# A diffusion transformer layer: turned rows beside turned activations, gathers three ahead, context first in the band group, router on rows that are not normalised

## What is computed

```python
def layer(x, cond):                      # once for the context tokens, once for the latent ones
    sh1, sc1, gt1, sh2, sc2, gt2 = split(silu(cond) @ w_ada + b_ada, 6)
    h = rms_norm(x, g_pre_attn) * (1 + sc1) + sh1
    qa, ka, va, qb, kb, vb = split(h @ w_in)         # 8 + 8 query heads, 2 + 2 key heads of 64
    qa, ka = rope(rms_norm(qa, g_qa)), rope(rms_norm(ka, g_ka))
    oa = attention(qa, ka, va)           # global: a latent token reads 512 latent keys + 128 cached
    ob = windowed(qb, kb, vb, sink)      # band of +-128 tokens + 128 cached keys, with a sink logit
    x = x + gt1 * rms_norm(concat(oa, ob) @ w_out, g_post_attn)
    h = rms_norm(x, g_pre_ffn) * (1 + sc2) + sh2
    aff = softmax(h @ w_router)                      # 16 experts
    g, idx = top_k(aff.T, cap)                       # cap 64 latent rows, 16 context rows an expert
    y = (silu(h[idx] @ w_gate) * (h[idx] @ w_up)) @ w_down * g
    return x + gt2 * rms_norm(scatter_add(y), g_post_ffn)
```

## Time and profile before

| | |
|---|---|
| median of the runs shown | 989.94 us |
| the profiled execution's own time | 991.05 us |
| its span in the profile | 989.2 us |
| PE busy | 916.5 us (93% of the span) |
| DVE, ACT, POOL busy | 336.8, 211.5, 125.4 us |
| mean DMA rate | 270 GB/s, 267 MB in all |
| mean granted TensorE clock | 0.966 of full speed |

### The profile page before, as it was taken

How to read it: one execution, slowest core, us unless ns; L and a number is a source line. 1 busy time by engine, 2 the same in 40 slices (tenths; PEclk the granted TensorE clock), 3 DMA queues, 4 the chain that set the end, 5 groups by cost and what they waited for, 6 DMA issues and landing times.

```text
span 989.2 us, 20007 instructions
## 1 busy us (share of the span) xinstructions
PE 916.5 (93%) x8581; PEld 451.1 (46%) x8581; DVE 336.8 (34%) x887; ACT 211.5 (21%) x497; POOL 125.4 (13%) x207
## 2 busy tenths in 40 slices
PE   3699999899999999459999999999999999999995
PEld 2345544677755555333444434443444344444431
DVE  2255534777877762731101110111011101110115
ACT  5122221567655541210000000000000000000002
POOL 1011100000000000021202220222022202220021
PEclk9899999799999998679999999999999999999998
DMA  9996340500000007839999999999999999999782
GB/s 361 352 378 221 140 170 1 208 1 2 2 1 23 22 23 295 321 137 352 353 403 393 393 395 407 393 393 394 408 393 392 393 409 393 392 391 411 289 292 107
DMA packets 77780, 267.09 MB, mean 270 GB/s; under 512 B 6360, under 2 KB 12040, under 8 KB 77736
## 3 DMA queue, kind: packets, MB, share of 16 engines
q1 hardware_dynamic: 65536, 247.61, 64.2%
q0 software_dynamic: 7088, 14.95, 5.8%
q10 hardware_dynamic: 5112, 3.93, 1.2%
HBM read 252.32 MB, written 14.16 MB: 269 GB/s over the span
## 4 chain that ended last, share of the span: by engine, by line
PE 55%; DVE 2%; ACT 1%; issue 0%; DMA 0%; POOL 0%; DVEq 0%; ACTq 0%
PE ps L747 33%; PE ps L759 17%; PE ps L725 1%; PE ps L794 1%; PE ps L789 1%; PE ps L832 0%; PE ps L827 0%; PE ps L727 0%; PE ps L664 0%; DMA reg<-rows_c,kt 0%; ACT reg L1056 0%; DVE ring L1502 0%; ACT ring L1098 0%; DVE kt L1396 0%; DVE ring L1509 0%
## 5 line engine op out<-in xcount | busy, mean ns | idle before, releaser
L747 PE MATMUL ps<-ring,reg 128*32 128x512 f32 x2048 | 231.2, 592 | 0.0
L759 PE MATMUL ps<-ring,reg 128*32 128x256 f32 x2048 | 124.1, 384 | 3.2 <-DVE reg L1455 2.2
L747 PEld LDWEIGHTS ps<-ring,reg 128*32 128x32 f32 x2048 | 66.5, 110 | 126.7 <-issue 116.0
L1470 DVE TENSOR_SCALAR reg<-ps,kt 128x512 f32<-128x512 f32 x15 | 11.3, 751 | 317.5 <-PE ps L747 317.5
L511 PE MATMUL ps<-ring,reg_qt 128*128 128x512 f32 x240 | 107.5, 602 | 6.5 <-DMA ring<-in_w_in 6.5
L759 PEld LDWEIGHTS ps<-ring,reg 128*32 128x32 f32 x2048 | 65.1, 111 | 68.2 <-issue 31.0
L1073 ACT ACTIVATE reg<-ps 128x256 f32<-128x256 f32 x16 | 6.1, 383 | 404.1 <-PE ps L789 404.1
L641 PE MATMUL ps<-ring,reg 128*128 128x512 f32 x160 | 78.8, 621 | 0.0
L511 PEld LDWEIGHTS ps<-ring,reg_qt 128*128 128x128 f32 x240 | 45.1, 193 | 60.1 <-issue 52.9
L1545 POOL TENSOR_TENSOR small<-small,mhalf 128x1 f32<-128x1 f32 (+2 forms) x30 | 23.0, 766 | 349.9 <-DVE small L1302 240.9
L1026 ACT ACTIVATE ring<-ps 128x640 f32<-128x640 f32 (+3 forms) x80 | 44.3, 553 | 67.7 <-PE ps L572 65.5
(11 more groups left out here) (200 smaller groups left out, 984.8 us busy)
## 6 DMA issues: line engine op xcount, KB each, us to landing
ring<-in_w_up SPq DMA_DIRECT2D x32, 2048.0 KB, 18.4
ring<-in_w_down SPq DMA_DIRECT2D x32, 2048.0 KB, 17.8
ring<-in_w_gate SPq DMA_DIRECT2D x16, 2048.0 KB, 15.7
reg_qt<-in_w_gate SPq DMA_DIRECT2D x16, 2048.0 KB, 16.1
ring<-in_w_ada SPq DMA_DIRECT2D x12, 2048.0 KB, 15.0
reg<-in_x_sample SPq DMA_DIRECT2D x8, 512.0 KB, 6.2
ring<-in_w_in SPq DMA_DIRECT2D x2, 2048.0 KB, 14.0
ring<-in_w_out SPq DMA_DIRECT2D x2, 2048.0 KB, 10.0
```

What stands on the lines that cost most here:

```text
L747: last = pe.matmul(o[64 * n + r:64 * n + r + 32, :], x[:, j, hf, r:r + 32], w[:, j, n * HALF:(n + 1) * HALF], start=(hf == 0 and j == 0), ...
L759: last = pe.matmul(o[32 * q:32 * q + 32, :], x[:, c % 2, c // 2, :], w[:, j, q * QUART:(q + 1) * QUART], start=(c == 0), stop=(c == KC - 1))
L1470: dve.tensor_scalar(y_l, ps[:, 3, :], g_l[:, bass.ds(e, 1)], None, ALU.mult)
```

## The change

Eight edits, in the order in which they run:

1. The small loads move from ACT's queue to SP's: seven ("keys") behind the first block of w_in, ten ("consts") behind the second. The first block of w_in comes in four DMAs and is awaited in two halves. `ADA_AFTER` moves its pieces one to two projections later.
2. `shift_to_logits` and `spread_shift` form the part of the logits that comes from the shift, and DVE folds the scale into the router's weights (`wrm`), so that logits = rstd * (x1 @ wrm) + bias. The signs are turned, so that a minimum takes the place of the maximum.
3. Group A runs four pairs of latent units and then one pair of context units, four times.
4. `OUT_ORDER` becomes 0, 1, 2, 3, 4. PE turns x1 itself, not the normalised rows; ACT copies it (`copy_x1`) where DVE modulated it. `route_logits` of three tiles moves into the units.
5. Each tile has its own softmax. The context's top 16 and its lists come before the last tile's norm. The last tile (latent 4) is squared, gated, added, turned and copied in halves. POOL takes over the means.
6. The latent top 64 runs after the last tile's affinities. On PE `cast_gate(1, ...)` stands ahead of the last `turn_aff`.
7. In an expert's step `turn_rows(e + 2)` follows the turned activations, so twelve transposes stand together; gathers run three experts ahead; DVE's `modulate` stands after `activations`.
8. `last_context` moves between the two halves of the last down product.

```diff
-ADA_AFTER = {2: 2, 5: 3, 8: 4, 11: 5}
+ADA_AFTER = {4: 2, 7: 3, 9: 4, 12: 5}
-OUT_ORDER = [1, 2, 3, 4, 0]
-HEAD_UNITS = ([(0, h, t) for t in range(TILES) for h in range(HEADS)]
+OUT_ORDER = [0, 1, 2, 3, 4]
+A_PAIRS = []
+for quarter in range(4):
+    A_PAIRS += [(2 * p, 1 + quarter) for p in range(PAIRS)] + [(2 * quarter, 0)]
+HEAD_UNITS = ([(0, h + i, t) for h, t in A_PAIRS for i in (0, 1)]
...
                     if m == 0:
-                        sp.dma_start(d[:, :, 0:256], w[:, :, 512:768]).then_inc(slot_in[slot_of(u)], 16)
-                        sp.dma_start(d[:, :, 256:512], w[:, :, 1280:1536]).then_inc(slot_in[slot_of(u)], 16)
+                        for b in (0, 1):
+                            k = slice(4 * b, 4 * b + 4)
+                            sp.dma_start(d[:, k, 0:256], w[:, k, 512:768]).then_inc(win0_in[b], 16)
+                            sp.dma_start(d[:, k, 256:512], w[:, k, 1280:1536]).then_inc(win0_in[b], 16)
+                        load_keys()
...
+                        if m == 1:
+                            load_consts()
...
+            def shift_to_logits():
+
+                pe.wait_ge(consts_in, 16 * N_CONSTS)
+                pe.wait_ge(modcol_ready, 4)
+                for c in range(KC):
+                    last = pe.matmul(ps[0:E, 7, 0:2], wr[:, c * E:(c + 1) * E], cmod[:, 2, :, c],
+                                     start=(c == 0), stop=(c == KC - 1))
+                last.then_inc(shift_turned, 1)
...
+                if o >= 2 and j == 7:
+                    route_logits(o - 2)
             turn_probs(n_units - 1)
             values(n_units // 2 - 1)
 
             project_out(4, 0, KC)
-            for o in range(3):
-                route_logits(o)
             turn_x1(3, 0)
+            turn_x1(3, 1)
+            turn_aff(0)
             project_out(4, KC, KC + 4)
-            turn_x1(3, 1)
+            route_logits(3)
+            turn_aff(1)
+            turn_aff(2)
             project_out(4, KC + 4, 2 * KC)
-            route_logits(3)
...
+            turn_aff(3)
+            pe.wait_ge(lists_c_ready, 1)
+            for a in (2, 3):
+                last = pe.transpose(ps[:, 1, a * E:(a + 1) * E], lists[:, a, :], ident[0:E, 0:E])
+            last.then_inc(lists_c_turned, 1)
             turn_x1(4, 0)
             turn_x1(4, 1)
             route_logits(4)
...
             for r in range(4):
                 cast_gate(1, r)
+            turn_aff(4)
...
                 product_l(2, U, xT_l[odd]).then_inc(up_a, 1)
-                if not final:
-                    turn_rows(e + 1)
                 weight_in(3, e)
...
                 if following:
                     pe.wait_ge(xe_ready, e + 2)
                     gate_product(*following, 0)
+                pe.wait_ge(y_ready, e + 1)
                 for j in range(2):
-                    last = pe.transpose(TC[:, QUART + j * P:QUART + (j + 1) * P], a_c[:, j * P:(j + 1) * P],
+                    last = pe.transpose(YC[:, QUART + j * P:QUART + (j + 1) * P], a_c[:, j * P:(j + 1) * P],
...
+                if ahead:
+                    pe.wait_ge(xe_ready, e + 2)
+                    turn_rows(e + 2)
                 if following:
                     gate_product(*following, 1)
-                pe.wait_ge(y_ready, e + 1)
...
                     product_l(4, Y, aT_l).then_inc(down_a, 1)
+                    last_context()
                     product_l(5, Y, aT_l).then_inc(down_b, 1)
...
             gate_product(0, 0, 0)
+            turn_rows(1)
             gate_product(0, 0, 1)
...
+            square_half(0)
+            exp_logits(3)
+            square_half(1)
+            square_x1_half(0)
+            square_x1_half(1)
             normalise_x1(4)
             store_rows(4)
...
+            def copy_x1_last(half):
+                o = TILES - 1
                 t = OUT_ORDER[o]
...
+                dve.wait_ge(x1_turned, 2 * o + half + 1)
+                dve.wait_ge(x1_squared, o + 2)
+                dve.tensor_copy(h2T[:, 4 * half:4 * half + 4, t * P:(t + 1) * P],
+                                out_at(o)[:, half, :].rearrange("p (c n) -> p c n", c=4)).then_inc(h2_ready, 1)
...
+            gate_half(1)
+            add_half(0)
+            add_half(1)
+            copy_x1_last(0)
+            copy_x1_last(1)
+            logits_of(4)
+            affinities(4)
+            dve.wait_ge(aff_turned, 2)
+            link(dve.tensor_copy(affs[0][:, LAT - P:LAT], ps[0:E, 7, 0:P]))
             for r in range(CAP_L // 8):
...
                 for odd in (0, 1):
-                    modulate(pair * 2 + odd + 1, 1 - odd)
                     activations(pair * 2 + odd)
+                    modulate(pair * 2 + odd + 2, odd)
                     weigh(pair * 2 + odd)
...
-            pool.wait_ge(xe_turned, 1)
-            gather(1)
+            for n in (1, 2):
+                pool.wait_ge(xe_turned, n)
+                gather(n)
...
-            with pool.Fori(0, E - 2) as e:
-                pool.wait_ge(xe_turned, e + 2)
-                gather(e + 2)
+            with pool.Fori(0, E - 3) as e:
+                pool.wait_ge(xe_turned, e + 3)
+                gather(e + 3)
                 scatter(e)
+            scatter(E - 3)
             scatter(E - 2)
```

More of the change, by code:

```diff
@@ L330, in build @@
         N_EARLY = 6
-        N_CONSTS = 17
-        LOADS = [sum((2 if UNITS[v][:2] == ("win", 0) else 1) for v in range(len(UNITS)) if slot_of(v) == s)
-                 for s in range(SLOTS)]
+        N_KEYS = 7
+        N_CONSTS = 10
+        LOADS = [sum(UNITS[v][:2] != ("win", 0) for v in range(len(UNITS)) if slot_of(v) == s) for s in range(SLOTS)]
         block = ctx.enter_context(nc.Block())
@@ L444, in landed @@
             def landed(u):
-                loads = sum((2 if UNITS[v][:2] == ("win", 0) else 1) for v in range(u + 1) if slot_of(v) == slot_of(u))
+                loads = sum(UNITS[v][:2] != ("win", 0) for v in range(u + 1) if slot_of(v) == slot_of(u))
                 pe.wait_ge(slot_in[slot_of(u)], 16 * loads)
@@ L643, in project_out @@
                                      start=(c == 0), stop=(c == KC - 1))
+                    if i == KC - 1 and o == TILES - 1:
+                        last.then_inc(o_half, 1)
                     if i == 2 * KC - 1:
@@ L666, in route_logits @@
-                last.then_inc(router_done, 1)
+                    pe.wait_ge(router_set, 3)
+                if o == TILES - 1:
+                    pe.wait_ge(logits_ready, o)
+                for c in range(KC):
+                    if c % 4 == 0:
+                        pe.wait_ge(h2_ready, 2 * o + (1 + c // 4 if o == TILES - 1 else 2))
+                    last = pe.matmul(dst, h2T[:, c, t * P:(t + 1) * P],
+                                     wrm[:, (KC * cond + c) * E:(KC * cond + c + 1) * E], start=(c == 0),
+                                     stop=(c == KC - 1))
@@ new lines, in route_logits, with turn_aff @@
+                last.then_inc(router_done, 1)
+            def turn_aff(o):
+                t = OUT_ORDER[o]
+                pe.wait_ge(aff_ready, o + 1)
+                if t in (0, 1):
+                    pe.wait_ge(exp_done, n_units)
+                if t == TILES - 1:
+                    pe.wait_ge(attn_ready, n_units // 2)
+                dst = ps[0:E, 1, 0:P] if t == 0 else ps[0:E, 7, 0:P] if t == TILES - 1 else ps[0:E, 0, (t - 1) * P:t * P]
+                last = pe.transpose(dst, expl[:, t, :], ident[:, :])
+                if t == 0:
+                    last.then_inc(aff_c_turned, 1)
+                if t >= TILES - 2:
+                    last.then_inc(aff_turned, 1)
@@ L706, in _ @@
             route_logits(4)
[L707 to L708 removed]
             for r in range(4):
                 cast_gate(1, r)
+            turn_aff(4)
             pe.wait_ge(lists_ready, 1)
[L712 to L713 removed]
+            for a in (0, 1):
+                last = pe.transpose(ps[:, 0, a * E:(a + 1) * E], lists[:, a, :], ident[0:E, 0:E])
             last.then_inc(lists_turned, 1)
@@ L771, in gate_product, with last_context, expert @@
                 product_l(s, G, xT_l[odd]).then_inc((gate_a, gate_b)[half], 1)
-            def expert(e, odd, following, final=False):
+            def last_context():
+                pe.wait_ge(put_on_ready, 1)
+                pe.wait_ge(y_copied_c, 1)
+                pe.wait_ge(silu_done, 2 * E)
+                pe.wait_ge(actT_l_ready, E)
+                for q in range(4):
+                    last = pe.matmul(ps[:, (0, 1, 2, 5)[q], 0:QUART], put_on_c[32 * q:32 * q + 32, :],
+                                     y_c[32 * q:32 * q + 32, :], start=True, stop=True)
+                last.then_inc(put_on, 1)
+            def expert(e, odd, following, ahead=True, final=False):
                 weight_in(2, e)
```

355 lines of the change are left out of this document (205 added, 150 removed).

## The result

| | before | after |
|---|---|---|
| median | 990.42 us | 976.89 us |
| lowest to highest | 989.48 to 991.17 | 975.98 to 979.38 |
| profiled execution, its span | 991.05, 989.2 us | 975.98, 974.2 us |
| mean granted clock | 0.966 | 0.981 |

The ratio is 0.9868, with a 95% interval of 0.9847 to 0.9888: 13.5 us faster, against 11.8 forecast.

What follows compares the result with a forecast made beforehand. PE was taken to bound projections, group B's projection stretch and experts (loads also near their limit there), small-step chains the rest. Terms -7.3 + 1.0 + 0.5 + 0.2 + 5.5 - 5.0 - 3.9 - 2.8 = -11.8 gave 978.1 us median, range 974 to 983.

Steps and rivals of the forecast that it cites:

- B: Rival at the start: the start doesn't move, 4 us of gain instead of 7.3 or less, 983; chance 0.15.
- C: Rival in the experts: the loads bind, so nothing is gained in the loop, 982; chance 0.15.
- D: Rival in the routing: it runs at full clock, -3.3 us more, 975; chance 0.15.
- Rival A: In attention: the clock falls at the context pairs, 3.4 us a fall, five falls giving 994; chance 0.07.
- The prediction's last line: The prediction is wrong if the clock falls in attention or a wait for `slot_in` shows up in the loop.
- Step 1: Start: small loads behind w_in let PE start at about 36.2, not 42.09, clock kept up; -7.3 us (bounds 4 and 9).
- Step 2: Router's shift: extra matmuls on the full PE, +1.0 us (bounds 0.5 and 2), and small DVE operations, +0.5.
- Step 3: Group A: context units some 6 us less, against half clock on latent units, 3.5 to 5; +0.2 us (bounds -4, +4).
- Step 4: Group B: context units alone, projections under tiles 1 to 4, three `route_logits` moved in; +5.5 us (bounds +2 and +9).
- Step 5: Routing, from `project_out(4)` to the row numbers: 50 us instead of 54.1, leaning to low clock; -5.0 (bounds -8.5 and -2).
- Step 6: Experts: joining two transpose groups saves 0.28 us, 14 times, -3.9 us (bounds -4.2 and 0); load margin just used up.
- Step 7: Tail: `last_onto(1)` starts earlier after the last product, -2.3 us, and at full clock, -0.5; together -2.8 (bounds -3.3 and -1.5).

Runs made afterwards that it cites:

- the rerun: The changed kernel, with no edit, run again beside the first three follow-up kernels: 977.92 us, ratio 0.9874 to the kernel before.
- Experiment 5: Against the changed kernel, ACT issues the small loads again behind its copies, the first weights still in halves: 983.97 us, ratio 0.9937.
- experiment 1: Against the changed kernel, PE turns the last affinities before the four `cast_gate` steps instead of after them: 974.59 us, ratio 0.9842.
- experiment 10: Against the 972.05 us kernel (casts last, unread routing products, loop placed), 8 of 16 products in the context's second down-projection half left out: 968.52 us.
- experiment 4: Against the changed kernel, `last_context` stands behind the last down product again: 979.09 us, ratio 0.9888.

## Why the prediction was right, and by how much

The sign was right and seven of the eight parts held to 1.0 us, group A not. The parts miss by 3.2 us in all between the profiled executions. The median, 976.89 for 978.1, misses by 1.2 and lies inside the forecast's own range. The case was mostly the forecast's: the start moved (B did not come), the loads didn't bind (C), the route and the casts ran at half clock (not D). Rival A did not come in the profile after. In the rerun the clock fell twice in attention, for 3.4 us each, at a price of 1.0 us in groups A and B together. The prediction's last line called itself wrong if the clock falls in attention at all; that sign was too sharp.

**Step 1** had the right time, 35.9 for 36.2, and half of the reason. It named both ACT's queue and the lower rate beside its loads (347 GB/s, not 406), and saw that the columns decide in the end, but it gave ACT's part no price of its own. Experiment 5 does: with the weights in halves the columns on ACT decide at 40.9, and the weights alone would have let PE start at 37.7. So of the 6.2 us, 1.2 come from the halves, 3.2 from ACT and 1.8 from weights that no longer come beside ACT's loads. The full clock at the start was forecast and came.

**Step 2**: the projections take 130.8 us against 131.9, with 1.7 us of clock regained, which leaves some 0.6 for the shift, forecast 1.0.

**Step 3** is the one that missed: -1.7 for +0.2, by two terms that cancel in part. The larger is the clock. I carried the stretch at half clock over to the latent units, at 3.5 to 5 us; it did not come in the profile after, and in the rerun it cost 0.3 us. Without that term the step says -3.3 to -4.8, which is more than was measured. So the other term was too large as well, the "some 6 us less" of the context units. It gives them 0.58 us each (10.6 less 6, by eight). Measured, on DVE, are the scaling of a latent unit, the same place one latent pair later, and the first context unit of two rounds that follow each other:

```profile
204.68 0.55 DVE L1488 TENSOR_SCALAR ring<-ring,small 128x640 f32<-128x640 f32 x1
209.04 0.55 DVE L1488 TENSOR_SCALAR ring<-ring,small 128x640 f32<-128x640 f32 x1
210.24 0.29 DVE L1488 TENSOR_SCALAR ring<-ring,small 128x128 f32<-128x128 f32 x1
229.52 0.29 DVE L1488 TENSOR_SCALAR ring<-ring,small 128x128 f32<-128x128 f32 x1
```

A latent pair takes 4.36 us, a round of four of them and one context pair 19.28, so the context pair takes 1.84, or 0.92 a unit. Against the 1.33 of the earlier trace rows that is 3.3 us for eight units, not 6. The step's number came nearer than its terms, and that is luck.

**Step 4** met its sum, +5.5, by two misses that cancel, which is luck too. The first eight units took 12.4 us for 11.2. The rest took 9.7 us more than before (107.3 less 97.6), where the terms add up to 10.9, of which 0.8 for the clock wasn't needed in this profile.

**Step 5**: 49.2 us for 50, and experiment 1 puts the casts' share at 3.3 to 3.9 us. A price of step 5 can thus be had back by the order of two lines.

**Step 6**: a turn is 0.57 us shorter, 0.29 an expert, for 0.28. The total is 3.3 for 3.9, and the 0.6 is the clock: half clock reaches 4.7 us into the first products, where it was 3.3, which costs 0.7. The first pair is 1.0 us longer (76.4 before, 77.4 after, from expert 0's first product to the loop's first branch). The rest of that is work moved forward, since it now turns the rows of three experts, 18 transposes and not 12, and the last pair comes back 0.9 shorter. Step 6 took the margin of the loads as just used up; experiment 10 agrees.

**Step 7**: -3.8 for -2.8. `last_onto(1)` starts 1.0 us after the last product, not 0.8 as step 7 had it, against 3.8 before; with the 0.7 of `last_context` that is -2.1, for -2.3, and experiment 4 gives 2.3 back. The rest, 1.7 us for 0.5, goes with the clock: one stretch of 5.5 us at half in place of 3.4 and 7.1. The step put the full clock down to the move, but in experiment 4 the stretch of 3.4 us stays away without it. So this term was met by something else, and what it is stays open.

## What to carry to other kernels

Read for each wait not only what ended it, but what would have ended it next: at the start two causes lay 1.2 us apart, and mending the later one alone brought only that of 6.2 us. Put what nobody waits for behind what starts a chain of small steps: the casts cost 3.3 us only by standing first. Check the parts of a term, not only the term: groups A and B each held two misses that cancelled in whole or in part. And before you believe a slowdown in a loop that an edit did not touch, look at the instruction queue's packets.

## What the hardware did that I had not expected

- A loop of 1603 PE instructions stays with the engine, with no instruction packet for some 400 us, or is fetched anew in each turn, 9 packets of 16 KB. In the places tried, which of the two comes hangs on where its first instruction stands. The price here is 10 us a turn: two pauses of PE of about 4.2 and 1.8 us, and the rest mostly at the half clock of that stretch.
- ACT, issuing a row of small loads beside a busy weight queue, was held 6.5 us by four of them; the four after them took 1.9.
- Two executions of the same program differ in where the clock falls in attention (no stretch, or two of 3.4 us), worth 1.0 us in groups A and B, as much as some of the terms of the sum.
